# Guest steps beside the RWKV pairs: state steps moved to the sample states' bank, the gate product to the front, and single steps let in within a stage

## What is computed

```python
def rwkv7_mixer(cols, shift0, S0, mu, w0, w2, a0, a2, g2, k_k, k_a, r_k, gn_g, gn_b):
    ...
    w_log = -jax.nn.softplus(-(w0 + jnp.tanh(wd) @ w2)) - 0.5
    decay = jnp.exp(-jnp.exp(w_log))
    a = jax.nn.sigmoid(a0 + ad @ a2)
    g = jax.nn.sigmoid(gd) @ g2
    ...
    def step(S, inp):
        rt, wt, kt, vt, kkt, at = inp
        sa = jnp.einsum('bhvk,bhk->bhv', S, -kkt)
        S = S * wt[:, :, None, :] + sa[..., None] * (kkt * at)[:, :, None, :] + vt[..., None] * kt[:, :, None, :]
        return S, jnp.einsum('bhvk,bhk->bhv', S, rt)
    ...
    y = head_norm(jnp.swapaxes(ys, 0, 1), gn_g, GN_EPS) + gn_b
    y = y + (jnp.sum(r * k * r_k, axis=-1, keepdims=True) * v).reshape(B, T, W)
    return y * g, S1, cols[:, -1]
```

## Time and profile before

| | us |
|---|---|
| median of 3 runs | 2201.48 |
| lowest and highest | 2189.54 and 2206.9 |
| profiled execution | 2201.78 |
| its span | 2200.1 |
| the four pairs and the tail of post(3) in it | 304.0 to 620.3 |

### The profile page before, as it was taken

The page is one execution under the profiler, slowest core; times in us unless marked ns, Lnnn a source line. Parts: engine busy times, 40 slices in busy tenths (PEclk is TensorE's granted clock), DMA queues, the critical chain, the costliest instruction groups (busy, mean ns, idle before and its releaser), DMA issues.

```text
span 2200.1 us, 35765 instructions
## 1 busy us (share of the span) xinstructions
PE 2073.8 (94%) x14513; PEld 1815.7 (83%) x14513; DVE 1533.7 (70%) x2655; ACT 758.0 (34%) x940; POOL 611.9 (28%) x515
## 2 busy tenths in 40 slices
PE   7999987767999989999999999999899999999997
PEld 7998866656547779889899889989899999999997
DVE  6426565565345898887998988897767666766676
ACT  5334433332121013334544445544322222222223
POOL 8143536250000000222232241222432233322330
PEclk9999977788999999999999999999999999999999
DMA  5121210011131114567797697779988888888873
GB/s 187 59 61 50 60 37 2 7 48 43 50 129 59 39 63 151 199 251 290 270 342 274 244 364 269 254 285 352 387 302 296 304 323 292 299 302 317 306 264 122
DMA packets 175771, 437.45 MB, mean 199 GB/s; under 512 B 12192, under 2 KB 92832, under 8 KB 165280
## 3 DMA queue, kind: packets, MB, share of 16 engines
q1 hardware_dynamic: 127552, 242.81, 31.8%
q0 software_dynamic: 36864, 134.23, 16.4%
q10 hardware_dynamic: 11232, 58.73, 6.5%
HBM read 368.57 MB, written 67.17 MB: 198 GB/s over the span
## 4 chain that ended last, share of the span: by engine, by line
PE 59%; DVE 11%; ACT 1%; issue 1%; DMA 0%; POOL 0%; ACTq 0%; DVEq 0%
PE bank L1900 29%; PE bank L1830 22%; PE bank L1839 3%; PE bank L1737 3%; DVE sc L2434 1%; DVE si L2433 1%; DVE si L2436 1%; DVE u_lo L2441 1%; DVE isel L2576 1%; DVE sv L2432 1%; DVE sv L2435 1%; PE bank L1780 1%; DVE sca L2447 1%; DMA sca<-in_pu_rows,pick 0%; ACT u_hi L1133 0%
## 5 line engine op out<-in xcount | busy, mean ns | idle before, releaser
L1830 PE MATMUL bank<-xhi,u_hi 128*128 128x448 f32 x1024 | 386.9, 378 | 9.7 <-DVE u_lo L2441 9.7
L1900 PE MATMUL bank<-w_hi,v_hi 128*128 128x448 f32 x1024 | 378.4, 370 | 5.5 <-DVE w_lo L2679 5.5
L1900 PE MATMUL bank<-w_lo,v_hi 128*128 128x448 f32 x1024 | 378.0, 369 | 0.0
L1900 PE MATMUL bank<-w_hi,v_lo 128*128 128x448 f32 x1024 | 377.9, 369 | 0.0
L1830 PE MATMUL bank<-xhi,u_lo 128*128 128x448 f32 x1024 | 376.4, 368 | 0.0
L1830 PE MATMUL bank<-xlo,u_hi 128*128 128x448 f32 x1024 | 376.2, 367 | 0.0
L761 POOL DMA_INDIRECT sca<-in_pu_rows,pick x128 | 172.8, 1350 | 728.3 <-DVE sdot L2447 445.0
L761 POOL DMA_INDIRECT rows_v<-in_pv,pick x128 | 197.4, 1542 | 440.7 <-DVE xs L2661 393.0
L2685 DVE TENSOR_TENSOR v_lo<-v_raw,v_hi 128x4096 fp32r<-128x4096 f32 x32 | 141.6, 4425 | 183.7 <-ACT v_hi L1194 183.7
L1194 ACT ACTIVATE v_hi<-v_raw 128x4096 fp32r<-128x4096 f32 x32 | 116.1, 3627 | 440.1 <-PE bank L1900 437.4
L1830 PEld LDWEIGHTS bank<-xhi,u_hi 128*128 128x128 f32 x1024 | 193.6, 189 | 25.4 <-issue 9.7
(11 more groups left out here) (632 smaller groups left out, 3522.5 us busy)
## 6 DMA issues: line engine op xcount, KB each, us to landing
u_raw<-in_pu SPq DMA_DIRECT2D x64, 1024.0 KB, 5.0
v_raw<-in_pv SPq DMA_DIRECT2D x32, 2048.0 KB, 16.8
act_scratch<-actb ACTq DMA_DIRECT2D x64, 448.0 KB, 6.0
gate_scratch<-gst ACTq DMA_DIRECT2D x14, 2048.0 KB, 9.1
wts<-act_scratch SPq DMA_DIRECT2D x32, 896.0 KB, 4.8
gring<-gate_scratch SPq DMA_DIRECT2D x32, 896.0 KB, 8.5
wring<-in_w_q SPq DMA_DIRECT2D x4, 2048.0 KB, 8.6
wp_raw<-in_w_in SPq DMA_DIRECT2D x7, 1024.0 KB, 5.4
```

The costliest lines, as they stand in the source:

```text
L1830: ins = mm(bank[b][:, 0:DS], lhsT, rhs[:, 0:DS], **on)
L1900: ins = mm(bank[c][:, 0:DS], lhsT, rhs[q][:, e, :], **on)
```

## The change

In the state chain the products move from bank 7 to bank 6, where the sample states stand. So the sample states have to be read out of bank 6 first: DVE does so as a step of its own (S2), and the state steps become S3 to S9. The waits on lora_out and kk_norm at c = 1, 3 and 4 are gone; one on kk_norm stands at the output contribution (S11). The gate product moves from S15 to S1, and ACT's copy of it to S1 as well; the sample states' product (S2) now waits for that copy ("gate_out"). In pairs 1 and 2 the preparation of the next pair starts two steps later (lora_decay S3, lora_rate S5, kk_sums S6; on DVE decay_sums S5, decay_diff S6, the reciprocal S8). And of the two steps after each stage one is now taken in the middle of it, between its blocks d = 1 and d = 2; in the merges one is taken between L1650/L1652 and L1660 on PE, and between the second and third block on ACT and DVE. The core of the diff (the same single steps stand at further places on ACT and DVE):

```diff
@@ -970,6 +970,8 @@
                     copy_job(next(jobs))
 
             def prep(p):
+                for _ in range(2 if p > 1 else 0):
+                    yield
                 lora(2 * p + 1, "sw", "w0", p)
                 yield
                 yield
...
@@ -984,6 +986,12 @@
                     yield
 
             def post(p):
+                act.wait_ge(S("gate_done"), p + 1)
+                if p:
+                    act.wait_ge(S("mix_ready"), 4 + p)
+                act.activation(X["gv"][:, 0:SEQ], bank[6][:, :], ACT.Copy)
+                act.activation(X["gv"][:, SEQ:NT], bank[7][:, 0:SAMP], ACT.Copy).then_inc(S("gate_out"), 1)
+                own(S("gate_out"))
                 for _ in range(13):
                     yield
                 act.wait_ge(S("gvar_done"), p + 1)
...
@@ -991,14 +999,7 @@
                 act.activation(X["d"][:, SEQ:NT], bank[7][:, 0:SAMP], ACT.Sqrt, bias=eps_t[:, 1:2], scale=1.0 / 64
                                ).then_inc(S("gstd_ready"), 1)
                 own(S("gstd_ready"))
-                yield
-                act.wait_ge(S("gate_done"), p + 1)
-                if p:
-                    act.wait_ge(S("mix_ready"), 4 + p)
-                act.activation(X["gv"][:, 0:SEQ], bank[6][:, :], ACT.Copy)
-                act.activation(X["gv"][:, SEQ:NT], bank[7][:, 0:SAMP], ACT.Copy).then_inc(S("gate_out"), 1)
-                own(S("gate_out"))
-                for _ in range(3):
+                for _ in range(4):
                     yield
 
             c_mg = 0
...
@@ -1038,6 +1039,8 @@
                                        bank[d][:, 0:384].rearrange("p (s a d) -> p s a d", s=2, a=3)[:, :, 0:2, :],
                                        ACT.Copy).then_inc(S("powers_ready"), 1)
                         own(S("powers_ready"))
+                        if d == 1:
+                            step()
                     if s < 2:
                         act.wait_ge(S("stage_done"), stage_no(p, s, 4))
                         act.activation(XS[s][:, 0:2, :], bank[5][:, 0:128].rearrange("p (a d) -> p a d", a=2), ACT.Copy
...
@@ -1377,35 +1382,36 @@
                     pe.wait_ge(S("bonus_ready"), p)
                 else:
                     pe.wait_ge(S("d_ready"), 4)
+                if p >= 2:
+                    pe.wait_ge(S("gate_out"), p - 1)
                 channel_product(p, w2[:, 128 * p:128 * p + 128], xwa[0:64, :], "lora_done", rest_of(p))
 
             def lora_rate(p):
                 pe.wait_ge(S("lora_out"), 2 * p + 1)
-                if p >= 2:
-                    pe.wait_ge(S("state_ready"), 8 * (p - 2) + 3)
                 channel_product(p, a2[64:128, 128 * p:128 * p + 128], xwa[64:128, :], "lora_done", rest_of(p))
 
             def kk_sums(p):
                 pe.wait_ge(S("lora_out"), 2 * p + 2)
                 pe.wait_ge(S("kk_squares"), p + 1)
-                if p >= 2:
-                    pe.wait_ge(S("state_ready"), 8 * (p - 2) + 4)
                 channel_product(p, blk[:, :], X["t"], "kk_summed", rest_of(p))
 
             def bonus_sums(p):
                 pe.wait_ge(S("chan_ready"), p + 1)
                 if p >= 2:
-                    pe.wait_ge(S("gate_out"), p - 1)
+                    pe.wait_ge(S("gstd_ready"), p - 1)
                 channel_product(p, blk[:, :], X["t"], "bonus_done", rest_of(1))
 
             def prep(p):
+                later = 2 if p > 1 else 0
+                for _ in range(later):
+                    yield
                 lora_decay(p)
                 yield
                 yield
                 lora_rate(p)
                 yield
                 kk_sums(p)
-                for _ in range(14):
+                for _ in range(14 - later):
                     yield
                 bonus_sums(p)
                 yield
...
@@ -1459,11 +1465,14 @@
                     mm(bank[6][:, :], lhsT, rhs[:, 0:SEQ], start=True, stop=True)
                     mm(bank[7][:, 0:SAMP], lhsT, rhs[:, SEQ:NT], start=True, stop=True).then_inc(S(name), 1)
                 pe.wait_ge(s_init, 16 * 10)
+                pe.wait_ge(S("bonus_ready"), min(p + 2, 4))
+                if p:
+                    pe.wait_ge(S("gstd_ready"), p)
+                main_and_rest(g2[:, pc], xg, "gate_done")
+                yield
                 pe.wait_ge(S("gh_copied"), 2 * p + 2)
                 pe.wait_ge(S("sample_copied"), 3 * p + 3)
-                pe.wait_ge(S("bonus_ready"), min(p + 2, 4))
-                if p:
-                    pe.wait_ge(S("gate_out"), p)
+                pe.wait_ge(S("gate_out"), p + 1)
                 for b in range(NB):
                     for h in range(2):
                         hs = slice(64 * h, 64 * h + 64)
...
@@ -1471,22 +1480,17 @@
                 ins.then_inc(S("sstep_done"), 1)
                 yield
                 for c in range(1, 8):
-                    pe.wait_ge(S("state_ready"), 8 * p + c)
-                    if p < 2 and c == 1:
-                        pe.wait_ge(S("lora_out"), 2 * (p + 2) + 1)
-                    if p < 2 and c == 3:
-                        pe.wait_ge(S("lora_out"), 2 * (p + 2) + 2)
-                    if p < 2 and c == 4:
-                        pe.wait_ge(S("kk_norm"), p + 3)
+                    pe.wait_ge(S("state_ready"), 9 * p + 1 + c)
                     o = 64 * (c % 2)
                     for h in range(2):
                         hs = slice(64 * h, 64 * h + 64)
-                        ins = mm(bank[7][hs, o:o + 64], Gt[q][hs, c, :], Sst[hs, c - 1, :], start=True, stop=True)
+                        ins = mm(bank[6][hs, o:o + 64], Gt[q][hs, c, :], Sst[hs, c - 1, :], start=True, stop=True)
                     ins.then_inc(S("state_step"), 1)
                     yield
                 yield
-                yield
                 pe.wait_ge(S("rstate_ready"), p + 1)
+                if p < 2:
+                    pe.wait_ge(S("kk_norm"), p + 3)
                 for c in range(1, 8):
                     for h in range(2):
                         hs = slice(64 * h, 64 * h + 64)
...
@@ -1505,10 +1509,7 @@
                 yield
                 pe.wait_ge(S("gsq_ready"), p + 1)
                 main_and_rest(blk[:, :], reff, "gvar_done")
-                yield
-                pe.wait_ge(S("gstd_ready"), p + 1)
-                main_and_rest(g2[:, pc], xg, "gate_done")
-                for _ in range(3):
+                for _ in range(4):
                     yield
 
             c_mg = c_md = 0
...
@@ -2057,8 +2061,9 @@
             def prep(p):
 
                 AR = ARP[p % 2]
-                yield
-                yield
+                later = 2 if p > 1 else 0
+                for _ in range(2 + later):
+                    yield
                 decay_sums(p)
                 yield
                 decay_diff(p)
...
@@ -2226,16 +2231,19 @@
                 dve.tensor_copy(Sst[:, 0, :], PH[q][:, 0, :]).then_inc(S("state_ready"), 1)
                 own(S("state_ready"))
                 yield
+                dve.wait_ge(S("sstep_done"), p + 1)
+                TT(SsS[:, :, :], bank[6][:, :].rearrange("p (c d) -> p c d", c=NB),
+                   EpE[:, p, 8:16].unsqueeze(2).to_broadcast([128, NB, 64]), ALU.mult).then_inc(S("state_ready"), 1)
+                own(S("state_ready"))
+                yield
                 for c in range(1, 8):
                     o = 64 * (c % 2)
                     dve.wait_ge(S("state_step"), 7 * p + c)
-                    STT(out=Sst[:, c, :], in0=bank[7][:, o:o + 64], scalar=EpE[:, p, c:c + 1], in1=PH[q][:, c, :],
+                    STT(out=Sst[:, c, :], in0=bank[6][:, o:o + 64], scalar=EpE[:, p, c:c + 1], in1=PH[q][:, c, :],
                         op0=ALU.mult, op1=ALU.add).then_inc(S("state_ready"), 1)
                     own(S("state_ready"))
-                    yield
-                dve.wait_ge(S("sstep_done"), p + 1)
-                link(TT(SsS[:, :, :], bank[6][:, :].rearrange("p (c d) -> p c d", c=NB),
-                        EpE[:, p, 8:16].unsqueeze(2).to_broadcast([128, NB, 64]), ALU.mult))
+                    if c < 7:
+                        yield
                 TT(SsS[:, :, :], SsS[:, :, :], PHS[q][:, :, :], ALU.add).then_inc(S("rstate_ready"), 1)
                 own(S("rstate_ready"))
                 yield
...
```

16 lines of the change are left out of this document (9 added, 7 removed).

## The result

| | before | after |
|---|---|---|
| median, us | 2193.05 (13 runs) | 2179.48 (13 runs) |
| lowest and highest | 2188.76 and 2206.9 | 2164.83 and 2188.8 |
| ratio, 95% interval | | 0.9921, 0.9899 to 0.9944 |
| profiled execution | 2201.78 | 2185.72 (span 2184.0) |

What follows compares the result with a forecast made beforehand. The prediction saw each pair as a chain going from engine to engine, none full, with PE waiting and its clock lowered. Waits of 14.7 us plus clock of 12.0 made 26.7 off the profiled 2201.8: 2175 us, range 2160 to 2198.

Steps and rivals of the forecast that it cites:

- (a): Pair 2: the sample states wait for ACT's two copies of the gate product; new wait 1.0 us, bounds 0.6 and 2.3.
- masks: Pair 2: the host's masks on DVE, delayed behind the gate's copy, cost PE 0.5 us.
- (b): Pair 2, stage 0: the wait for the first sigmoids on ACT is partly covered; 1.1 us is left.
- (c): Pair 2, stages 0 and 1: DVE's queue puts decay_sums and decay_diff ahead of Sst updates; 1.2 us, bounds 0 and 2.1.
- (d): Pair 2, stage 2: a state step waits for Sst behind DVE's reciprocal of 3.75 us; 3.7 us, bounds 0.8 and 6.
- (e): Pair 2: AR's products on DVE before stage 3 lengthen the mean's wait for y from 1.0 to 1.9 us.
- (f): Pair 2, merge: PE waits for ACT's table load, root and one copy; 2.3 us, the old wait under a new name.
- (g): Pair 2: DVE's second reciprocal ends nearer to the host's last merges; wait of 0.8 us.
- both stretches: Heads of pairs 1 and 2: two stretches at 1.2 GHz, 16.9 and 13.0 us, taken as gone, worth 12.0 us.
- Rival 1: The waits only change place and one half-clock stretch stays or returns; 2190 us, chance 24%.
- Rival 2: The clock holds in later parts of pairs 1 to 3 too, 12 us more won; 2163 us, chance 17%.
- Rival 3: Slower: the long wait behind the reciprocal drops the clock through most of pairs 1 and 2; 2219 us, chance 6%.
- Rival 4: Nothing visible: each removed wait returns in the next, the clock stays as before; 2200 us, chance 9%.

Runs made afterwards that it cites:

- f1: The changed kernel with matrix products that nobody reads put on PE ahead of three waits of pairs 1 to 3; 2169.80 us, ratio 0.9894.
- c1: The changed kernel with DVE's guest steps taken post before prep, so the update of Sst goes ahead of the preparation's scan and reciprocal; 2172.22 us, ratio 0.9902.
- c2: The changed kernel with ACT's guest step in each merge taken behind the four copies of TB; 2166.46 us, ratio 0.9886.
- d1: The changed kernel with the reciprocal of the keys' norm left out in pairs 1 to 3 (result wrong, only time counts); 2171.47 us, ratio 0.9899.

## Why the prediction was right, and where not

**Time and direction.** 2175 against 2179.48 us, inside the forecast's own 2167 to 2183. Part of that is luck: 26.7 us were taken from 2201.8, but over 13 runs the kernel before has its median at 2193.05, 8 us below that of the three runs on hand then. The gain was 13.6 us by the medians and 17 by the ratio. In the profiled execution, where identical code can be compared, 26.7 us were forecast for the pairs and 19.5 came.

**The waits: 14.7 forecast, 11.3 measured** (10.3 without the gate product at the end of pair 3). For pair 2 by its letters, in after and in f1, whose PE runs at full clock to the middle of the pair:

| | forecast | after | f1 |
|---|---|---|---|
| (a) gate's copy | 1.0 | 0.94 | filled |
| masks | 0.5 | 0.86 | filled |
| (b) first sigmoids | 1.1 | 0 | 1.01 |
| (c) queue, state steps | 1.2 | 0 | 0.68 and 1.22 |
| (d) reciprocal | 3.7 | 4.94 | 3.54 |
| SsS | | 0 | 0.47 |
| (e) mean | 1.9 | 2.38 | 1.91 |
| (f) root | 2.3 | 2.12 | 2.13 |
| (g) last merges | 0.8 | 1.23 | 1.23 |

The forecast adds up to 12.5, and so does after. Pairs 1 and 2 came out as forecast, within 0.3 us (4.0 and 5.7 of idle less where 4.3 and 5.9 were named). One by one the terms fit f1 better than after: (b) and (c) were worked out for a PE at full clock, and they show as soon as it has it. In after PE at half clock covers them, and (d), (e) and (g) are larger by as much; that the sums agree is partly luck. That decay_exps cost nothing under (d) held, and c1 shows the other half of the sentence: without the cover 2.4 us of them are paid. Pair 3 gave 2.6 and not 3.8, and 1.0 of the 2.6 is the gate product in the wait at its end, for which the prediction booked nothing: (a), the Sst waits, y and the root were 0.94, 0.46 + 0.51, 0.53 and 0.85 against 1.0, 0.5 + 0.7, 0.6 and 1.0, but the last merges 2.4 in place of 0.6. Pair 0 gave a loss of 1.0, not a gain of 0.7: the sigmoid's wait fell from 2.32 to 1.01 and the two waits behind the reciprocal from 6.7 to 5.0, but 2.9 and 1.4 us for POOL's squares and products came, an engine that I had dismissed with "its result is asked for at S18"; that holds for pairs 1 and 2, not for pair 0.

**The tail: nothing.** 0.2 us lost, with the wait for mixT at 2.19 us: the product left, and the wait grew by as much, as forecast.

**The clock: the step that failed.** It says of the new waits "none above 1.2 us, so I take both stretches as gone". They did not go. They were 16.9 and 13.0 us long with 13.08 and 8.86 us of work, and are 10.2 and 10.1 us long with PE busy throughout. Taking half of the busy time in a low stretch as its cost, they cost 11.0 us before and 10.2 after, so 0.8 was won of the 12.0 that the step booked. The price, 0.40 us for each half-clock us, was fair (11.0 for 29.9); that the stretches go was wrong. One reading behind it was off as well: the wait of 2.7 us for rw_t doesn't stand inside the two stretches but behind them, ended at 394.3 and 470.8 us. Windows of the kernel before, its other low stretches in pairs 1 and 2 (but for that at the start of pair 1), which I had left as they are:

```profile
394.70:398.10 3.40, 2.98 (x40) 2.98 (x42) 3.29 (x2) 0.38 (x1) 0.00 (x0) 0.50 0.00 0
408.40:418.60 10.20, 8.32 (x112) 7.07 (x114) 5.10 (x12) 0.77 (x3) 3.70 (x3) 0.50 0.10 31
425.40:428.90 3.50, 3.50 (x69) 3.50 (x70) 3.43 (x3) 1.70 (x5) 0.00 (x0) 0.51 0.00 0
486.90:493.70 6.80, 5.76 (x70) 4.52 (x69) 3.17 (x6) 0.76 (x3) 0.46 (x1) 0.50 0.86 285
500.50:503.95 3.45, 3.45 (x67) 3.45 (x68) 3.38 (x3) 1.70 (x5) 0.00 (x0) 0.51 0.02 7
```

They hold 24.0 us of work; the four of after hold 12.6. By halves that is 5.7 us, and with the 0.8 an estimate of 6.5, where pairs 1 and 2 lost 5.6 us of busy time. Pairs 0 and 3 gave 2.6 more (3.8 without the gate product's work in pair 3). So 12.0 was 8.2, or 9.4, and mostly from other places. Why the head stretches stayed is open: the step took them as gone because no new wait was above 1.2 us, and in the kernel after both stood behind waits of 2.06, 0.94 and 0.86 us; but with the same three waits c1, c2 and d1 have heads at full clock as well. The clock was 0.85 and 0.88 in pairs 1 and 2 where near 0.9 was named, and the pairs 70.1 and 68.5 us long where 66 to 68 was. f1 also shows a fault of the sum's form: terms of clock and of waits aren't independent, since nearly half of a gain of clock returns as waits.

**The rule on table loads.** The Trainium skill (ScalarE: Activation LUTs, "What ACT_TABLE_LOAD costs") puts a drain of 1380 ns beside each load. The trace doesn't agree: behind each load in the pairs of the kernel after, the activation starts 0.01 to 0.02 us after its end (460.70 + 1.28, then 462.00), so the 8.3 us that the drains would have added weren't in the pairs. The load itself, 1.28 us, counts where something stands behind it: in the timeline of pair 2 the host's last two copies stand behind kk_root's, and in c1 behind that of decay_exps.

**The rivals.** Rival 1's 2190 us is close to what e1 measured, 2188.68: the change without its single steps. Rival 2's mechanism, more clock in the later parts, came in place of the forecast's own. Rival 3 didn't: (d) reached 4.9 us, and the clock behind it was low for 3.4 us only (467.8 to 471.2). Rival 4, no effect, is out by the interval, which ends at 0.9944.
